# Score matmuls stacked to full contraction height, and vector work reordered, in a fused encoder layer

## The chip, the cores and the metric

One core of a Trainium2 chip runs one program, launched once. The metric is the device time of a run in microseconds (us); each kernel has several runs and their median is given. A profile is one more execution with every instruction recorded.

## What is computed

One encoder layer on x (1 x 1024 x 2048, float32): an RMSNorm, one input projection whose columns feed three mixers, a gate on each mixer, an output projection added to x, and a last RMSNorm.

```python
h = _rmsnorm(x, norm_g[l])
proj = jnp.einsum('bsd,de->bse', h, w_in[l])
ua, va, ga, q, k, v, gb, xc, gc = jnp.split(proj, pts, axis=-1)
ya = _spatial_gating(ua, va, ...)            # 4 groups x 128 channels
yb = _swa_sink_attention(q, k, v, b_sinks[l], rel_bias)
yc = _multiscale_pool(xc, c_w_pool[l], c_scale[l])
mix = jnp.concatenate([ya * silu(ga), yb * silu(gb), yc * silu(gc)], axis=-1)
x = x + jnp.einsum('bse,ed->bsd', mix, w_out[l])
return _rmsnorm(x, final_g)
```

The attention has 16 query heads on 4 key/value heads, 64 channels each. A query chunk of 64 positions sees its own chunk and the one before it, with a relative bias and a sink logit per head:

```python
logits = jnp.einsum('bcqkgd,bcjkd->bckgqj', qb, kb) * 64 ** -0.5 + bias
m = jnp.maximum(jnp.max(logits, -1, keepdims=True), sink)
p = jnp.exp(logits - m)
p = p / (jnp.sum(p, -1, keepdims=True) + jnp.exp(sink - m))
out = jnp.einsum('bckgqj,bcjkd->bcqkgd', p, vb)
```

## The kernel before

**Precision.** TensorE (PE) multiplies fp32r operands. Each float32 operand is split in two: ScalarE (ACT) rounds it to a high part (`split_hi`, L812; `x_hi`, L830) and VectorE (DVE) subtracts to get the low part (`split_lo`, L1106; `x_lo`, L1111). Each product is then three matmuls (`three`, L1561 to L1563): high by high, high by low, low by high.

**Order of the work.** A sequence of 104 groups J of weights (2048 columns of 128 rows) is written out by hand. All engines loop over J, and each executes what its own loop lists, in that order. While PE works on group J, ACT and DVE split group J + 1. Groups 0 to 23 are the first half of the sequence positions (512), 24 to 47 the second half. In a half, g = J mod 24: g = 0 to 3 make k and v, g = 4 to 19 make a tile of q (even g) or of its gate (odd g), g = 20 to 23 a part of mixer A. Groups 48 to 103 are the rest of the projections, and the output projection, done over both halves at once by Strassen-Winograd's seven products: four pairs p = 0 to 3 of 14 steps each, so J = 48 + 14 p + j. Two steps make a product, in the order A12, A11, S2, S1, S4, S3, A22. Each step goes through the four PSUM banks `N[st]`, st = 0 to 3, with 12 matmuls a bank; the odd step ends the product of a bank.

**Banks.** Before the even step of the next product PE waits, bank by bank, until DVE has added the bank into its result (`bank_free` waits on `y_added`). DVE does that in `add_chain`: banks 0 to 2 in the odd step in which PE ends them, bank 3 at the start of the next step. In group 103 the order is different (`last_product`): PE does banks 0 and 1 of groups 102 and 103, then banks 2 and 3 of both, and DVE adds a bank at a time, each followed by ACT's square, the root, and the scaled output rows (`finish_second`).

**Jobs.** The sums of operand blocks that the products need are made along the way by `job`, at groups fixed in the tables `X_AT`, `M_AT` and `S_AT`. A job of kind "s" (r = 0 to 7) makes four sums and splits three tiles, and one of kind "t" splits the other two, one group later (for r = 6 and 7 in the same group). A job of kind "m" splits one tile. The parts go from the buffer `stage` to DRAM by DMAs that the SP queue issues in the next group, and the next job may write `stage` when these have landed (`wait_stored`). SP also loads four operand blocks for each step (`load_s`, 2 MB), the weights, and the tiles `residual` of x, which `add_residual` adds on DVE in steps 8, 11 and 13 of pairs 2 and 3.

**Attention.** At g = 4 the two k tiles (128 rows, two kv heads each) are split (`k_tile_hi`, `k_tile_lo`), and each q tile of two heads at the odd g behind it (`q_tile_hi`, `q_tile_lo`). At the end of the groups g = 5 to 20 PE does `scores` of a piece (two blocks of 128 queries of two heads, 32 pieces in all): for each block three products of 64 rows, for the two heads side by side in the upper and lower rows of the array, 12 matmuls. One group later come its four transposes (`transpose`), two later 16 matmuls with v (`values`). Within a group the order on PE is: projection, values, transposes, scores. DVE brings the scores to `logits` in four instructions (L1292), then maximum and normalisation around ACT's exponentials.

**Start and end.** The sum of squares of x is made by ACT's squares (`x_square`) and GpSimd's (POOL's) sums (L742); ACT may be at most two squares ahead of POOL; the last six squares are in ACT's loop at J = 1, and `split_hi(3)` is among them. `finish_first`, at group 102, scales the finished first half of the rows: a root on ACT, a reciprocal on DVE, then eight scalings on ACT and eight on DVE.

Of the kernel before, what the change touches and what calls it, by code (L numbers as in the profile page):

```python
# [14 lines left out]
P = 128  # L15
# [66 lines left out]
S_AT = (36, 40, 44, 48, step(PAIR_A, 5), step(PAIR_A, 8), step(PAIR_O, 1), step(PAIR_O, 2))  # L82
# [102 lines left out]
def build(nc, x, x_t, w, w_b, norm_g, ln_g, ln_b, w_s, b_s, sinks, rel_bias, one_hot, inv_count, w_pool,  # L185
# [8 lines left out]
    with ExitStack() as ctx:  # L194
# [41 lines left out]
        k_hi = place("k_hi", [P, 2, CHUNK + HS], F32R)  # L236
        k_lo = place("k_lo", [P, 2, CHUNK + HS], F32R)
        at[0] = at_attn + 2 * 4 * KV_HEADS * (CHUNK + HS)
# [485 lines left out]
        def _(pool):  # L724
# [14 lines left out]
            for half in range(HALVES):  # L739
                for kt in range(1, KT):  # L740
                    pool.wait_ge(x_sq_done, KT * half + kt + 1)
                    pool.tensor_tensor(acc[half], acc[half], x_sq[:, kt % 2, :], ALU.add  # L742
                                       ).then_inc(x_acc_done, 1)
                    pool.wait_ge(x_acc_done, (KT - 1) * half + kt)
                if half == 0:
                    pool.wait_ge(consts_loaded, 16 * 10)
                for n in range(PIECES):
                    m = PIECES * half + n
                    if m >= 1:
                        pool.wait_ge(exp_done, 4 * m)  # L750
                    pool.tensor_copy(logits[:, :, P:P + 1].rearrange("p (h t) s -> p h (t s)", t=2),
                                     sink_sb[:, 2 * (n // 2):2 * (n // 2) + 2].unsqueeze(2).broadcast_to([P, 2, 2])
                                     ).then_inc(sink_set, 1)
# [3 lines left out]
        def _(sc):  # L757
# [95 lines left out]
            def k_tile_hi(half, pair):  # L853

                if half == 1:

                    sc.wait_ge(k_saved, 2)
                sc.wait_ge(t_evac, T_TILES * half + pair + 1)
                sc.activation(k_hi[:, pair, CHUNK:CHUNK + HS], k_stage[pair][:, 0:HS], ACT.Copy).then_inc(k_hi_done, 1)

            def q_tile_hi(half, i):
# [6 lines left out]
                sc.activation(q_stack[:, 0, :], q_t[:, 0:HS], ACT.Copy).then_inc(q_hi_done, 1)  # L868
# [112 lines left out]
            for J in range(TOTAL):  # L981
# [12 lines left out]
                if 4 <= J + 1 < TOTAL:  # L994
# [87 lines left out]
                if J == step(PAIR_O + 1, 12):  # L1082
# [9 lines left out]
        def _(ve):  # L1092
# [128 lines left out]
            def add_residual(p, k):  # L1221
# [60 lines left out]
            def softmax_scores(half, n):  # L1282
# [6 lines left out]
                for c in range(2):  # L1289
                    rows = slice(64 * c, 64 * c + 64)  # L1290
                    for a in range(2):
                        last = ve.scalar_tensor_tensor(  # L1292
                            out=logits[rows, 2 * a:2 * a + 2, 0:P],
                            in0=S_bank[a][rows, :].rearrange("p (t s) -> p t s", t=2)[:, :, 64 * c:64 * c + P],
                            scalar=DH ** -0.5, in1=bias[rows, 2 * i + a, :].unsqueeze(1).broadcast_to([64, 2, P]),
                            op0=ALU.mult, op1=ALU.add)
                last.then_inc(scaled, 1)
                ve.wait_ge(scaled, m + 1)
                if half == 0 and tp == 0:

                    settle(ve.memset(logits[0:64, 0:4:2, 0:64], -1e30))
# [4 lines left out]
            def k_tile_lo(half, pair):  # L1306
                ve.wait_ge(k_hi_done, 2 * half + pair + 1)
                ve.tensor_tensor(k_lo[:, pair, CHUNK:CHUNK + HS], k_stage[pair][:, 0:HS],
                                 k_hi[:, pair, CHUNK:CHUNK + HS].bitcast(F32), ALU.subtract).then_inc(k_lo_done, 1)

            def q_tile_lo(half, i):

                ve.wait_ge(q_hi_done, 8 * half + i + 1)
                ve.tensor_tensor(q_stack[:, 1, :], q_t[:, 0:HS], q_stack[:, 0, :].bitcast(F32), ALU.subtract
                                 ).then_inc(q_lo_done, 1)
# [89 lines left out]
            for J in range(TOTAL):  # L1405
# [41 lines left out]
                if half < HALVES and is_t(g - 1):  # L1447
                    ve.wait_ge(group_done, J)
                    if g - 1 == G_Q:

                        ve.wait_ge(k_lo_done, 2 * (half + 1))
# [83 lines left out]
                if p >= 0 and j % 2 == 1 and J < TOTAL - 1:  # L1535
                    add_chain(*divmod((J - IN_GROUPS) // 2, PRODUCTS), range(ST - 1))
# [9 lines left out]
                if J == step(PAIR_O + 1, 12):  # L1546
# [8 lines left out]
        def _(pe):  # L1555
# [184 lines left out]
            def scores(half, n):  # L1740
                i, tp, m = n // 2, n % 2, PIECES * half + n
                pe.wait_ge(q_lo_done, 8 * half + i + 1)
                if n == 0:
                    pe.wait_ge(k_lo_done, 2 * (half + 1))
# [6 lines left out]
                for tl in range(2):  # L1751
                    q0 = P * (2 * tp + tl)
                    for k, (q_part, k_part) in enumerate(((0, k_hi), (0, k_lo), (1, k_hi))):
                        for a in range(2):
# [14 lines left out]
            def values(half, n):  # L1769
# [6 lines left out]
                for tl in range(2):  # L1776
                    st = 2 * tp + tl
                    for a in range(2):
                        kv = 2 * (i // 4) + a
                        d, at = slice(64 * kv, 64 * kv + 64), (2 * a + tl) * P  # L1780
# [130 lines left out]
```

## Time and profile before

| | us |
|---|---|
| median of 3 runs | 1253.82 (1252.9 to 1254.21) |
| the profiled execution: its own time | 1252.9 |
| its span in the trace | 1251.1 |
| PE busy | 1230.0 (98% of the span) |
| PE weight loads busy | 1014.3 (81%) |
| DVE busy | 831.2 (66%) |
| ACT busy | 498.8 (40%) |
| POOL busy | 54.9 (4%) |
| the 16 DMA engines | 69.2% of the span, 251 GB/s |

The profiled execution's own time is 1.8 us above its span. PE's clock was granted in full nearly throughout (0.997 in the mean). Matmuls overlap in the records, so that the distance between two starts, not the length of one, says what a matmul costs.

### The profile page before, as it was taken

To read this page: it belongs to the slowest core of one execution; us is meant where nothing else is said; L and a number is where in the kernel's file an instruction comes from. 1 tells how busy PE (TensorE), PEld (TensorE's weight loads), DVE (VectorE), ACT (ScalarE), POOL (GpSimd) and SP (SyncE) were. 2 spreads that over 40 slices of the span, in tenths; PEclk is the share of its full clock that TensorE was granted. 3 is DMA by queue.
4 is the path that set the end of the run, shared out by engine and by line. 5 is a ranking of instruction groups with operands and counts; after the bars stand their busy time and mean duration, and the time that the engine had idled before them with its cause. 6 is when DMAs were issued, how large, how long until landed. Compare 5 with 4: busy or idle time off the path is not lost.

```text
span 1251.1 us, 16376 instructions
## 1 busy us (share of the span) xinstructions
PE 1230.0 (98%) x6310; PEld 1014.3 (81%) x6310; DVE 831.2 (66%) x1115; ACT 498.8 (40%) x887; POOL 54.9 (4%) x70
## 2 busy tenths in 40 slices
PE   7999999999999999999999999999999999999996
PEld 6878888888988888888888887888888888888884
DVE  7657666664576577776376568777678755665556
ACT  7435454435553354454334112333333512323135
POOL 3400000003110000000000000000000000000000
PEclk9999999999999999999999999999999999999998
DMA  8499446353655256565896877659999799855769
GB/s 312 128 311 332 146 163 210 141 184 124 220 189 211 102 182 222 185 216 201 335 343 225 322 299 270 214 189 356 415 350 354 296 351 395 305 202 204 284 223 332
DMA packets 98813, 314.16 MB, mean 251 GB/s; under 512 B 10128, under 2 KB 13232, under 8 KB 87344
## 3 DMA queue, kind: packets, MB, share of 16 engines
q1 hardware_dynamic: 98736, 313.12, 69.2%
q8 instruction: 50, 0.82, 0.3%
q14 instruction: 27, 0.22, 0.1%
HBM read 241.77 MB, written 71.30 MB: 250 GB/s over the span
## 4 chain that ended last, share of the span: by engine, by line
PE 95%; DMA 2%; DVE 1%; ACT 1%; issue 1%; SPq 0%; ACTq 0%; DVEq 0%
PE n_bank L1561 17%; PE n_bank L1563 17%; PE n_bank L1562 17%; PE t_bank L1561 11%; PE t_bank L1562 10%; PE t_bank L1563 10%; PE e_bank L1561 2%; PE n_bank L1756 2%; PE e_bank L1563 2%; PE e_bank L1562 2%; PE n_bank L1782 2%; PE n_bank L1766 1%; DMA raw<-w_dram 1%; PE e_bank L1796 1%; PE e_bank L1806 1%
## 5 line engine op out<-in xcount | busy, mean ns | idle before, releaser
L1106 DVE TENSOR_TENSOR w_lo<-raw,w_hi 128x1024 fp32r<-128x1024 f32 (+1 forms) x116 | 138.0, 1228 | 153.2 <-ACT w_hi L812 152.9
L1561 PE MATMUL t_bank<-op_hi,w_hi 128*128 128x512 f32 x512 | 203.1, 397 | 0.0
L1562 PE MATMUL t_bank<-op_lo,w_hi 128*128 128x512 f32 x512 | 199.7, 390 | 0.0
L1563 PE MATMUL t_bank<-op_hi,w_lo 128*128 128x512 f32 x512 | 199.4, 389 | 0.0
L812 ACT ACTIVATE w_hi<-raw 128x1024 fp32r<-128x1024 f32 (+1 forms) x116 | 113.2, 1021 | 167.1 <-PE t_bank L1563 111.5
L1561 PE MATMUL n_bank<-s_ring,w_hi 128*128 128x512 f32 x448 | 178.0, 397 | 0.0
L1563 PE MATMUL n_bank<-s_ring,w_lo 128*128 128x512 f32 x448 | 174.4, 389 | 0.0
L1562 PE MATMUL n_bank<-s_ring,w_hi 128*128 128x512 f32 x448 | 174.3, 389 | 0.0
L1561 PE MATMUL n_bank<-w_hi,s_ring 128*128 128x512 f32 x448 | 174.3, 389 | 0.0
L1562 PE MATMUL n_bank<-w_lo,s_ring 128*128 128x512 f32 x448 | 174.3, 389 | 0.0
L1563 PE MATMUL n_bank<-w_hi,s_ring 128*128 128x512 f32 x448 | 174.3, 389 | 0.0
L1561 PEld LDWEIGHTS t_bank<-op_hi,w_hi 128*128 128x128 f32 x512 | 96.3, 188 | 20.5
L1563 PEld LDWEIGHTS t_bank<-op_hi,w_lo 128*128 128x128 f32 x512 | 96.1, 188 | 20.7
L1562 PEld LDWEIGHTS t_bank<-op_lo,w_hi 128*128 128x128 f32 x512 | 96.5, 188 | 17.9
L1562 PEld LDWEIGHTS n_bank<-s_ring,w_hi 128*128 128x128 f32 x448 | 84.1, 188 | 19.1 <-issue 1.9
L1561 PEld LDWEIGHTS n_bank<-s_ring,w_hi 128*128 128x128 f32 x448 | 84.1, 188 | 19.0 <-issue 1.9
L1563 PEld LDWEIGHTS n_bank<-s_ring,w_lo 128*128 128x128 f32 x448 | 84.1, 188 | 17.6
L1562 PEld LDWEIGHTS n_bank<-w_lo,s_ring 128*128 128x128 f32 x448 | 84.1, 188 | 17.6
L1561 PEld LDWEIGHTS n_bank<-w_hi,s_ring 128*128 128x128 f32 x448 | 84.1, 188 | 17.6
L1563 PEld LDWEIGHTS n_bank<-w_hi,s_ring 128*128 128x128 f32 x448 | 84.1, 188 | 17.3
L812 ACT ACTIVATE w_hi<-x_w 128x1024 fp32r<-128x1024 f32 x48 | 48.2, 1051 | 115.0 <-PE n_bank L1563 112.7
L1106 DVE TENSOR_TENSOR w_lo<-x_w,w_hi 128x1024 fp32r<-128x1024 f32 x48 | 56.6, 1219 | 46.3 <-ACT w_hi L812 46.0
(225 smaller groups left out, 1825.7 us busy)
## 6 DMA issues: line engine op xcount, KB each, us to landing
s_ring<-x_parts SPq DMA_DIRECT2D x112, 512.0 KB, 6.1
s_ring<-m_parts SPq DMA_DIRECT2D x112, 512.0 KB, 6.0
raw<-w_dram SPq DMA_DIRECT2D x46, 1024.0 KB, 5.1
y_w<-w_b_dram SPq DMA_DIRECT2D x16, 1024.0 KB, 11.2
mix<-x_t_dram SPq DMA_DIRECT2D x56, 256.0 KB, 5.0
m_parts<-stage SPq DMA_DIRECT2D x24, 512.0 KB, 7.6
x_parts<-stage SPq DMA_DIRECT2D x32, 256.0 KB, 3.0
x_parts<-mix SPq DMA_DIRECT2D x32, 256.0 KB, 3.0
```

Of the source, the lines that this page charges most:

```text
L812: sc.activation(w_hi[:, J % 2, part], w_source(J)[:, part], ACT.Copy).then_inc(hi_done, 1)
L1106: ve.tensor_tensor(w_lo[:, J % 2, part], w_source(J)[:, part], w_hi[:, J % 2, part].bitcast(F32), ALU.subtract).then_inc(lo_done, 1)
L1561: pe.matmul(psum_out, stat[0], mov[0], start=first, stop=False)
L1562: pe.matmul(psum_out, stat[0], mov[1], start=False, stop=False)
L1563: return pe.matmul(psum_out, stat[1], mov[0], start=False, stop=last)
L1756: mm = pe.matmul(S_bank[a][:, 256 * tl:256 * tl + WINDOW], q_stack[rows, q_part, q0:q0 + P], k_part[rows, i // 4, q0:q0 + WINDOW], start=k ...
L1766: mm = pe.transpose(PT_bank[:, P * b:P * b + P], logits[:, b, 0:P], ident[:])
L1782: mm = pe.matmul(O_bank[64 * a:64 * a + 64, P * tl + 64 * c:P * tl + 64 * c + 64], vals[:, st, d], probs_t[:, at + 64 * c:at + 64 * c + 64 ...
L1796: mm = pe.matmul(E[0][:, P * st:P * st + P], mix[:, M_A + j, P * st:P * st + P], w_s_sb[:, j, :], start=True, stop=True)
L1806: pe.matmul(E[1][:], w_pool_sb[:, j, :], aux[:, HIST:HIST + HS], start=True, stop=True).then_inc(pool_ready, 1)
```

## The change

Seven edits, in one diff. The scores take operands of 128 rows: `q_stack` holds for each head the high part of q in its own 64 rows and the low part in the other 64, and `k_hi` and `k_lo` hold each kv head's part in both halves of the rows, so that two matmuls a head and block give all four products of the parts; 8 matmuls a piece. The splits of k and q write 64 rows at a time. The scores are brought to `logits` in two instructions. The wait and place of `split_hi(3)` change. `add_chain` of banks 0 to 2 stands behind the jobs and the residuals in DVE's loop. One job "s" (and its "t") moves a group later. `finish_first` moves from group 102 to 101.

```diff
-S_AT = (36, 40, 44, 48, step(PAIR_A, 5), step(PAIR_A, 8), step(PAIR_O, 1), step(PAIR_O, 2))
+S_AT = (36, 40, 44, 48, step(PAIR_A, 6), step(PAIR_A, 8), step(PAIR_O, 1), step(PAIR_O, 2))
...
-        k_hi = place("k_hi", [P, 2, CHUNK + HS], F32R)
-        k_lo = place("k_lo", [P, 2, CHUNK + HS], F32R)
+        k_hi = place("k_hi", [P, KV_HEADS, CHUNK + HS], F32R)
+        k_lo = place("k_lo", [P, KV_HEADS, CHUNK + HS], F32R)
...
-                sc.activation(k_hi[:, pair, CHUNK:CHUNK + HS], k_stage[pair][:, 0:HS], ACT.Copy).then_inc(k_hi_done, 1)
+                for a in range(2):
+                    for to in (a, 1 - a):
+                        sc.activation(k_hi[64 * to:64 * to + 64, 2 * pair + a, CHUNK:CHUNK + HS],
+                                      k_stage[pair][64 * a:64 * a + 64, 0:HS], ACT.Copy).then_inc(k_hi_done, 1)
...
-                sc.activation(q_stack[:, 0, :], q_t[:, 0:HS], ACT.Copy).then_inc(q_hi_done, 1)
+                for a in range(2):
+                    rows = slice(64 * a, 64 * a + 64)
+                    sc.activation(q_stack[rows, a, :], q_t[rows, 0:HS], ACT.Copy).then_inc(q_hi_done, 1)
...
-                if 4 <= J + 1 < TOTAL:
+                if 3 <= J + 1 < TOTAL:
                     split_hi(J + 1)
...
                     for kt in range(KT - SQUARES_LAG, KT):
                         x_square(0, kt)
-                        if kt == KT - 4:
-                            split_hi(3)
...
-                if J == step(PAIR_O + 1, 12):
+                if J == step(PAIR_O + 1, 11):
                     finish_first()
...
                 elif k == 1:
-                    ve.wait_ge(y22_added, 8 * p + 2 * ST - 1)
-                elif p < PAIRS - 1:
-                    ve.wait_ge(y_added, added(p, Q_A22, ST - 2))
+                    ve.wait_ge(y22_added, 8 * p + ST)
                 else:
                     ve.wait_ge(y_added, added(p, Q_S3, ST - 1))
...
+                    last = ve.scalar_tensor_tensor(
+                        out=logits[rows, :, 0:P],
+                        in0=n_banks[rows, 0:2, :].rearrange("p t (a s) -> p (t a) s", a=2)[:, :, 64 * c:64 * c + P],
...
             def k_tile_lo(half, pair):
...
+                for a in range(2):
+                    own = slice(64 * a, 64 * a + 64)
+                    ve.wait_ge(k_hi_done, 8 * half + 4 * pair + 2 * a + 1)
+                    for to in (a, 1 - a):
+                        ve.tensor_tensor(k_lo[64 * to:64 * to + 64, 2 * pair + a, CHUNK:CHUNK + HS],
+                                         k_stage[pair][own, 0:HS],
+                                         k_hi[own, 2 * pair + a, CHUNK:CHUNK + HS].bitcast(F32),
+                                         ALU.subtract).then_inc(k_lo_done, 1)
...
+                for a in range(2):
+                    ve.wait_ge(q_hi_done, 16 * half + 2 * i + a + 1)
+                    own, other = slice(64 * a, 64 * a + 64), slice(64 - 64 * a, 128 - 64 * a)
+                    ve.tensor_tensor(q_stack[other, a, :], q_t[own, 0:HS], q_stack[own, a, :].bitcast(F32),
+                                     ALU.subtract).then_inc(q_lo_done, 1)
...
-                if p >= 0 and j % 2 == 1 and J < TOTAL - 1:
-                    add_chain(*divmod((J - IN_GROUPS) // 2, PRODUCTS), range(ST - 1))
                 for t, kind, i in JOBS:
                     if t == J:
                         job(kind, i)
                 for k, t in enumerate((8, 11, 13)):
                     if p >= PAIR_O and j == t:
                         add_residual(p, k)
+                if p >= 0 and j % 2 == 1 and J < TOTAL - 1:
+                    add_chain(*divmod((J - IN_GROUPS) // 2, PRODUCTS), range(ST - 1))
...
-                for tl in range(2):
-                    q0 = P * (2 * tp + tl)
-                    for k, (q_part, k_part) in enumerate(((0, k_hi), (0, k_lo), (1, k_hi))):
-                        for a in range(2):
-                            rows = slice(64 * a, 64 * a + 64)
-                            mm = pe.matmul(S_bank[a][:, 256 * tl:256 * tl + WINDOW], q_stack[rows, q_part, q0:q0 + P],
-                                           k_part[rows, i // 4, q0:q0 + WINDOW], start=k == 0, stop=k == 2)
+                for a in range(2):
+                    for tl in range(2):
+                        q0 = P * (2 * tp + tl)
+                        for part in (k_hi, k_lo):
+                            mm = pe.matmul(S_bank[tl][:, 256 * a:256 * a + WINDOW], q_stack[:, a, q0:q0 + P],
+                                           part[:, 2 * (i // 4) + a, q0:q0 + WINDOW], start=part is k_hi,
+                                           stop=part is k_lo)
```

The layout of `logits` changes from head by block to block by head with it (the sink's copy on POOL, the masked quarter, and `values` follow), and the counts of the semaphores follow the new numbers of instructions. `finish_first` moves in both ACT's and DVE's loop.

## Rows read from the trace of the kernel before

**Rows 1.** The page's fourth part: the chain that ended last, by engine.

```profile
PE 95%; DMA 2%; DVE 1%; ACT 1%; issue 1%; SPq 0%; ACTq 0%; DVEq 0%
```

**Rows 2.** Busy time by stretch: the last 34 us.

```profile
1217.00:1251.10 34.10, 21.85 (x97) 17.76 (x95) 21.80 (x37) 20.80 (x40) 0.00 (x0) 0.89 0.91 333
```

**Rows 3.** Timeline of PE: start, length, line, operation; one attention piece (n=2).

```profile
118.09 0.66 PE L1766 MATMUL n_bank<-ident,probs 128*128 128x128 f32 x4
118.68 0.36 PE L1756 MATMUL n_bank<-k_hi,q_stack 64*128 64x192 f32 x2
118.87 0.28 PE L1756 MATMUL n_bank<-k_lo,q_stack 64*128 64x192 f32 x2
...
119.32 0.28 PE L1756 MATMUL n_bank<-k_hi,q_stack 64*128 64x192 f32 x2
119.53 0.50 PE L1561 MATMUL t_bank<-op_hi,w_hi 128*128 128x512 f32 x1
119.86 0.39 PE L1562 MATMUL t_bank<-op_lo,w_hi 128*128 128x512 f32 x1
```

**Rows 4.** Timeline of PE: transposes with no scores behind them.

```profile
289.90 0.66 PE L1766 MATMUL n_bank<-ident,probs 128*128 128x128 f32 x4
...
290.63 0.39 PE L1562 MATMUL e_bank<-w_lo,op_hi 128*128 128x512 f32 x1
```

**Rows 5.** Timeline of PE: matmuls of 256 columns and 128 rows.

```profile
13.01 0.28 PE L1561 MATMUL n_bank<-w_hi,op_hi 128*128 128x256 f32 x1
13.13 0.28 PE L1562 MATMUL n_bank<-w_lo,op_hi 128*128 128x256 f32 x1
```

**Rows 6.** Last square on ACT; POOL's 15 sums; PE's first matmul of group 3.

```profile
43.54 0.64 ACT L851 ACTIVATE x_sq<-mix 128x512 f32<-128x512 f32 x1 [1.30 <-POOL rstd_row L742]
...
L742 POOL TENSOR_TENSOR rstd_row<-rstd_row,x_sq x15: 1297/1627/2295, 19.4 to 44.9; 128x512 f32<-128x512 f32 x15
...
43.67 0.28 PE L1561 MATMUL n_bank<-w_hi,op_hi 128*128 128x256 f32 x1
```

**Rows 7.** Low part of q on DVE and the scores behind it, group 29.

```profile
377.93 0.69 DVE L1314 TENSOR_TENSOR q_stack<-q_t,q_stack 128x512 fp32r<-128x512 f32 x1 [0.77 <-ACT q_stack L868]
...
381.80 0.36 PE L1756 MATMUL n_bank<-k_hi,q_stack 64*128 64x192 f32 x2
```

**Rows 8.** PE's first matmuls of groups 70 and 102, 32 groups apart.

```profile
868.76 0.39 PE L1561 MATMUL n_bank<-s_ring,w_hi 128*128 128x512 f32 x1
...
1216.93 0.39 PE L1561 MATMUL n_bank<-w_hi,s_ring 128*128 128x512 f32 x1
```

**Rows 9.** Issue to landing: the store issued at 858.4, the residual at 1217.9.

```profile
DMA to landing us min/median/max: 8.3/8.3/8.3
...
DMA to landing us min/median/max: 8.6/8.6/8.6
```

**Rows 10.** Timeline of DVE in groups 71, 75, 77, 89 and 103.

```profile
891.02 1.29 DVE L1127 TENSOR_TENSOR c<-c,stage 128x512 f32<-128x512 f32 x2 [2.34 <-ACT stage L881]
...
936.39 0.69 DVE L1127 TENSOR_TENSOR stage<-t,stage 128x512 fp32r<-128x512 f32 x1 [0.28 <-ACT stage L881]
...
953.88 0.68 DVE L1127 TENSOR_TENSOR stage<-t,stage 128x512 fp32r<-128x512 f32 x1
...
960.41 0.68 DVE L1185 TENSOR_TENSOR t<-n_bank,t 128x512 f32<-128x512 f32 x1
...
1085.83 2.29 DVE L1235 TENSOR_TENSOR t<-t,residual 128x2048 f32<-128x2048 f32 x1 [1.28 <-DMA residual<-x_dram]
...
1228.35 2.29 DVE L1235 TENSOR_TENSOR y<-y,residual 128x2048 f32<-128x2048 f32 x1
...
1232.89 0.68 DVE L1185 TENSOR_TENSOR y<-n_bank,y 128x512 f32<-128x512 f32 x1
```

**Rows 11.** Timeline of ACT: the table load and the scaling in group 102.

```profile
1222.27 1.28 ACT L783 ACT_TABLE_LOAD   x1
...
1224.11 2.56 ACT L790 ACTIVATE t<-t,rstd_y 128x512 f32<-128x512 f32 x4 [0.25 <-DVE rstd_y L1365]
```

More of the change, by code:

```diff
@@ L750, in _ @@
                         pool.wait_ge(exp_done, 4 * m)
-                    pool.tensor_copy(logits[:, :, P:P + 1].rearrange("p (h t) s -> p h (t s)", t=2),
-                                     sink_sb[:, 2 * (n // 2):2 * (n // 2) + 2].unsqueeze(2).broadcast_to([P, 2, 2])
+                    pool.tensor_copy(logits[:, :, P:P + 1].rearrange("p (t h) s -> p t (h s)", t=2),
+                                     sink_sb[:, 2 * (n // 2):2 * (n // 2) + 2].unsqueeze(1).broadcast_to([P, 2, 2])
                                      ).then_inc(sink_set, 1)
@@ L1290, in softmax_scores @@
                     rows = slice(64 * c, 64 * c + 64)
-                    for a in range(2):
[L1292 to L1296, printed above, removed]
+                    last = ve.scalar_tensor_tensor(
+                        out=logits[rows, :, 0:P],
+                        in0=n_banks[rows, 0:2, :].rearrange("p t (a s) -> p (t a) s", a=2)[:, :, 64 * c:64 * c + P],
+                        scalar=DH ** -0.5,
+                        in1=bias[rows, 2 * i:2 * i + 2, :].rearrange("p a s -> p (a s)").unsqueeze(1).broadcast_to([64, 2, 2 * P]),
+                        op0=ALU.mult, op1=ALU.add)
                 last.then_inc(scaled, 1)
@@ L1299, in softmax_scores @@
                 if half == 0 and tp == 0:
-                    settle(ve.memset(logits[0:64, 0:4:2, 0:64], -1e30))
+                    settle(ve.memset(logits[0:64, 0:2, 0:64], -1e30))
                 ve.wait_ge(sink_set, m + 1)
@@ L1306, in k_tile_lo @@
             def k_tile_lo(half, pair):
-                ve.wait_ge(k_hi_done, 2 * half + pair + 1)
-                ve.tensor_tensor(k_lo[:, pair, CHUNK:CHUNK + HS], k_stage[pair][:, 0:HS],
-                                 k_hi[:, pair, CHUNK:CHUNK + HS].bitcast(F32), ALU.subtract).then_inc(k_lo_done, 1)
-            def q_tile_lo(half, i):
-                ve.wait_ge(q_hi_done, 8 * half + i + 1)
-                ve.tensor_tensor(q_stack[:, 1, :], q_t[:, 0:HS], q_stack[:, 0, :].bitcast(F32), ALU.subtract
-                                 ).then_inc(q_lo_done, 1)
+                for a in range(2):
[6 more added lines that the diff above has]
+                                         ALU.subtract).then_inc(k_lo_done, 1)
+            def q_tile_lo(half, i):
+                for a in range(2):
[3 more added lines that the diff above has]
+                                     ALU.subtract).then_inc(q_lo_done, 1)
             def softmax_norm(half, n):
@@ L1449, in _ @@
                     if g - 1 == G_Q:
-                        ve.wait_ge(k_lo_done, 2 * (half + 1))
+                        ve.wait_ge(k_lo_done, 8 * (half + 1))
                     take(half, g - 1, q_t[:, 0:HS] if (g - 1 - G_Q) % 2 == 0 else pre[:, 0:HS])
@@ L1545, in _ @@
                         weigh(i)
-                if J == step(PAIR_O + 1, 12):
+                if J == step(PAIR_O + 1, 11):
                     finish_first()
@@ L1741, in scores @@
                 i, tp, m = n // 2, n % 2, PIECES * half + n
-                pe.wait_ge(q_lo_done, 8 * half + i + 1)
+                pe.wait_ge(q_lo_done, 16 * half + 2 * i + 2)
                 if n == 0:
-                    pe.wait_ge(k_lo_done, 2 * (half + 1))
+                    pe.wait_ge(k_lo_done, 8 * (half + 1))
                     pe.wait_ge(v_evac, ST * (half + 1))
@@ L1748, in scores @@
                     pe.wait_ge(scaled, m)
-                for tl in range(2):
-                    q0 = P * (2 * tp + tl)
-                    for k, (q_part, k_part) in enumerate(((0, k_hi), (0, k_lo), (1, k_hi))):
-                        for a in range(2):
-                            rows = slice(64 * a, 64 * a + 64)
-                            mm = pe.matmul(S_bank[a][:, 256 * tl:256 * tl + WINDOW], q_stack[rows, q_part, q0:q0 + P],
-                                           k_part[rows, i // 4, q0:q0 + WINDOW], start=k == 0, stop=k == 2)
+                for a in range(2):
[5 more added lines that the diff above has]
+                                           stop=part is k_lo)
                 mm.then_inc(s_ready, 1)
@@ L1779, in values @@
                         kv = 2 * (i // 4) + a
-                        d, at = slice(64 * kv, 64 * kv + 64), (2 * a + tl) * P
+                        d, at = slice(64 * kv, 64 * kv + 64), (2 * tl + a) * P
                         for c, vals in enumerate((v_prev, v)):
```

1 line of the change is left out of this document (removed).

## The prediction

> **What bounds the kernel.** I read the page's chain first: 95% of what ended last is PE [rows 1]. The stretches come next. From 8.4 to 1217 us PE has no long gap, so until then only what shortens PE's stream or makes it wait counts; in the last 34 us PE is busy for 21.9, and the end belongs to DVE and ACT [rows 2]. Then the timeline of PE around one attention piece, to price the scores [rows 3 to 5]. Last, what each PE group waits for, and how late DVE comes to it: the change alters DVE's order in the odd steps, and PE's bank wait stands behind each of them. Group starts are 10.88 apart: from 868.76 (group 70) to 1216.93 (group 102) are 32 of them [rows 8]. So group 72 starts at 890.52, 76 at 934.04, 78 at 955.80, 90 at 1086.37.
>
> **Scores on PE.** From the start of the transposes at 118.09 to the second projection matmul behind the scores at 119.86 pass 1.77 us [rows 3]. Where no scores stand between, the same way takes 290.63 - 289.90 = 0.73 [rows 4]. So a piece costs 1.04, though its six side-by-side pairs are only 0.11 apart (118.87 to 119.32 is four of them) [rows 3]. The other 0.37 sits around the borders: the first pair comes 0.19 before the second, and the first projection matmul takes 0.33 to the second instead of 0.23. I read it as the price of going from 128 rows to 64 and back. The new piece has 8 matmuls of 128 rows and 192 columns. No such one is in the trace; the four transposes (128 columns) pass at 0.10 each [rows 4], 256 columns at 0.12 [rows 5]. I take 0.11, since 192 lies between: 0.88, a gain of 0.16 in each of 32 pieces, 5.0 us. The ends: 8 x 0.10 gives 7.7, 8 x 0.12 gives 2.6.
>
> The Trainium skill speaks against this edit: TensorE: Matmul & The Clock Gate, Part 3 (Packing small matmuls), says that matmuls of few rows in different row groups run concurrently, at nearly the price of one. By that alone full rows lose, 8 slots for 6. TensorEngine Tiling (Array Packing), Key Properties, has the other side, "Mode switching requires drain". The trace shows both, pairs that start together and 0.37 at the borders; which weighs more is a matter of the rows above, and the first page alone is a rival below.
>
> **Splits of k and q.** Instructions of 64 rows are taken as long as those of 128 (0.69 on DVE, 0.60 from start to start, as the two in 1.29 show [rows 10]). At g = 4 DVE has eight instead of two, ACT eight instead of two; DVE is done 6 x 0.60 = 3.6 later. In group 4 the slack covers it. In group 28 DVE has a layer norm behind it and no idle time until q: today the low part of q ends at 378.6, and the scores start at 381.80 [rows 7]. It starts 3.6 later, waits about 0.77 for ACT as now, and has a second instruction: 378.6 + 3.6 + 0.6 = 382.8. PE would come at 381.7, half a border sooner than now: a stall of 1.1 (0 to 1.5). In the other q groups over 5 us of slack hide 0.6 on each engine. Two instead of four instructions for the scores lie beside PE: nothing.
>
> **split_hi(3).** PE needs group 3 at 43.67 [rows 6]. The last square starts at 43.54, held by POOL; POOL's sums took up to 2.30 when DVE worked beside them and 1.30 at best [rows 6]. The split now comes behind it. Without the split between, the last three sums are some 2 us faster together: last square 41.5, high part from 42.1 to 43.1, the low part's first half (1.2 to 2.1 on DVE) by 45.0. Stall 1.4; if POOL gains nothing, 44.1 + 1.1 + 2.1 = 47.3 and 3.6; at best 0.6.
>
> **Adds behind jobs and residuals.** `add_chain` frees bank 0 for PE at the next even step. Where DVE waits for a transfer first, PE now waits too.
> - *Group 70* (job t4, now in group 69). The stage must be free: the store of s4 is issued at 858.4, and one issued then landed 8.3 later [rows 9]: 866.7. ACT and DVE need 0.66 and 1.29 more, the two adds 1.28: 869.9. By the offset in group 71 (first split 891.02, 11.4 after its group's start) it is 871.8. PE wants 868.76: stall 1.1 to 3.1, taken 2.2.
> - *Group 72* (t5). The splits end at 892.3 [rows 10], an add is 0.68: 892.9 against 890.52, 2.4. The stores of t4 now come a group later and hold s5 by about 0.5 more; taken 2.6 (0.8 to 3.2).
> - *Group 76* (m14, m15). Their low parts end at 937.0 [rows 10], the add at 937.7 against 934.04: 3.7 (3.3 to 4).
> - *Group 78* (s6, t6). The jobs run from 953.88 to 960.41, 6.5 [rows 10]. They now start about 6.0 after group 77's start; 6.0 + 6.5 + 0.7 = 13.2 against 10.88: 2.3 (1.5 to 3). This one is no transfer, but DVE's own length.
> - *Group 90.* The residual lands at 1085.8, its add takes 2.29, then 0.68: 1088.8 against 1086.37 [rows 10]: 2.4 (2 to 2.8).
> - Groups 62 and 88 have work before the adds too, but the transfers are in, and PE's need is over 0.9 later: nothing. DVE's later work has over 4 us of slack at every split. Job s4 at the even step 68 lies before nothing that PE needs soon.
>
> **The end.** In group 101 the sums of squares are ready. ACT's table load (1.28) goes ahead of its wait. Its eight scalings take 2 x 2.5 [rows 11] and run until about 1221.4, ahead of `split_hi(103)`, so that split's low part is ready at 1223.7, and PE needs it at 1216.93 + 2 x 2.72 = 1222.37: a stall of 1.4. It costs the end little: PE's last matmul today starts before DVE's last adds, by 4 us. DVE is free for the last residual at 1224.9, which was issued at 1217.9 and lands 8.6 later, 1226.5 [rows 9]; today its add starts at 1228.35, and bank 0 at 1232.89 [rows 10]. So the chain of the last four banks (3.3 each) starts 1.85 earlier; bank 2, delayed on PE, comes to the same point. Gain 1.85 (0.9 to 2).
>
> **Sum.** -5.0 for scores, +1.1 and +1.4 in the first stages, +2.2 + 2.6 + 3.7 + 2.3 + 2.4 = +13.2 at the banks, -1.85 at the end: +8.85. On the profiled execution's own 1252.9 that is 1261.7. It stood 0.9 below the median; the forecast is 1262.
>
> **Rivals.**
> - *Transfers land sooner (the other side).* Every stage store and the residual land in a time that the trace gives for one layout of traffic. PE's delay spreads that traffic, and stores that land 3.7 earlier in a group would let the jobs end before PE asks. Then groups 70, 72, 76 and 90 lose nothing: 10.9 less, 1251, and with group 3's stall gone too 1249. For it: each stall leaves the queues more time. Against: SP issues the stores when PE starts a group, so they move with PE. It decides at a landing under 4.6 from the issue; the trace has 8.3 to 10.
> - *Borders stay.* The 0.37 is not from the rows in use but from scores as such. Then 8 x 0.11 replaces 6 x 0.11, +0.22 x 32 = +7.1 instead of -5.0: 1274. For it: pairs that start 0.11 apart cost no more than one matmul would. Against: the transposes give way to 128-row matmuls with no border at all [rows 4]. This rival is what Part 3 of the Trainium skill's page TensorE: Matmul & The Clock Gate would make of the edit.
> - *DVE passes through the jobs faster*, by a job's wait that was idle time of ACT and is no more: half of the bank stalls. Then 1255.5, hardly to be told from before.
>
> **Chances.** The forecast's case 0.80, own range 1256.5 to 1266.5 (the ends of the terms taken together, not all at once). Sooner transfers 0.09, borders 0.04, faster jobs 0.07. Faster by over 0.2% (2.5 us, about what a measurement can tell) 0.07, within 0.11, slower 0.82. The range 1255 to 1267 leaves out the first two rivals.
>
> **What would show it.** Scores: 8 matmuls 0.11 apart, and 0.23 from the first projection matmul to the second. PE's idle time ahead of the first matmuls of groups 70, 72, 76, 78, 90 with DVE's add as releaser, and of group 3's split. Banks of 0 stall at 76 and 90 would make the prediction wrong at once; so would scores that cost over 1 us. A stall before the scores of group 29 decides the k split, and bank 0's last add before 1232 plus the shift the end.

## The result, and the profile after

| | before | after |
|---|---|---|
| median in the comparison on one chip, us | 1253.53 | 1274.67 (1270.99 to 1276.23) |
| ratio | | 1.0165, 95% interval 1.014 to 1.0188 |
| profiled execution: own time, span | 1252.9, 1251.1 | 1271.56, 1269.7 |

The change costs 21.1 us; 1262 was forecast, with 1255 to 1267 as the range. The direction was right, the size was not: the loss is more than twice the forecast one. A wait of PE is in what follows the distance between the matmuls on either side of it, less the 0.23 at which they otherwise follow each other. Line numbers differ by a few after the change: L1568 to L1570 are the three matmuls, L1187 is DVE's addition of a bank.

The chain that ended last now holds less PE than in [rows 1], 80%:

```profile
PE 80%; DMA 7%; DVE 5%; ACT 3%; issue 2%; POOL 1%; SPq 1%; ACTq 0%; DVEq 0%; POOLq 0%
```

What PE waited for, total, times, longest (waits view of after):

```profile
PE n_bank L1568 <- DVE t L1187: 12.1, 5, 3.9
PE n_bank L1568 <- DVE op_lo L1113: 8.2, 1, 8.2
PE n_bank L1568 <- DVE w_lo L1108: 2.5, 2, 1.3
PE n_bank L1762 <- DVE q_stack L1321: 2.3, 1, 2.3
```

The second line is the start of the kernel. The five waits of the first line stand at groups 70, 72, 76, 78 and 90, as forecast.

The attention piece of [rows 3]. The scores are 0.11 apart, and the projection matmul behind them takes 0.25 to the next, not 0.33:

```profile
119.43 0.66 PE L1773 MATMUL n_bank<-ident,probs 128*128 128x128 f32 x4
119.84 0.34 PE L1762 MATMUL n_bank<-k_hi,q_stack 128*128 128x192 f32 x1
120.02 0.27 PE L1762 MATMUL n_bank<-k_lo,q_stack 128*128 128x192 f32 x1
120.13 0.28 PE L1762 MATMUL n_bank<-k_hi,q_stack 128*128 128x192 f32 x1
...
120.80 0.42 PE L1568 MATMUL t_bank<-op_hi,w_hi 128*128 128x512 f32 x1
121.05 0.39 PE L1569 MATMUL t_bank<-op_lo,w_hi 128*128 128x512 f32 x1
```

From the transposes to that second matmul pass 121.05 - 119.43 = 1.62, against 1.77: 0.15 less in each piece. Only the first score stands further from the next (119.84 to 120.02, 0.18), as before the change (0.19).

Group 29, DVE and then PE. Before, DVE had two instructions for k_lo and one for q_stack [rows 7]:

```profile
369.59 2.84 DVE L1311 TENSOR_TENSOR k_lo<-q_t,k_hi 64x512 fp32r<-64x512 f32 x4
372.46 2.84 DVE L1311 TENSOR_TENSOR k_lo<-x_raw,k_hi 64x512 fp32r<-64x512 f32 x4
...
382.48 1.40 DVE L1321 TENSOR_TENSOR q_stack<-q_t,q_stack 64x512 fp32r<-64x512 f32 x2 [0.77 <-ACT q_stack L872]
```

```profile
381.27 0.39 PE L1570 MATMUL e_bank<-op_hi,w_lo 128*128 128x512 f32 x1
383.94 0.36 PE L1762 MATMUL n_bank<-k_hi,q_stack 128*128 128x192 f32 x1 [2.29 <-DVE q_stack L1321]
...
385.33 0.68 PE L1568 MATMUL t_bank<-op_hi,w_hi 128*128 128x512 f32 x1
385.81 0.63 PE L1569 MATMUL t_bank<-op_lo,w_hi 128*128 128x512 f32 x1
```

Four instructions of 64 rows take 2.84, the last one 0.69 of it, so they start 0.72 apart, where 0.60 was assumed. PE waits 2.67 - 0.23 = 2.4. Then it is slow: the last two matmuls stand 0.48 apart instead of the 0.25 above. The stretches tell why (start and end, length, PE busy, PE loads, DVE, ACT, POOL, granted clock, DMA share, GB/s; first of before, then of after):

```profile
376.00:393.00 17.00, 17.00 (x84) 13.84 (x84) 12.21 (x21) 6.22 (x13) 0.19 (x1) 1.00 0.81 310
```

```profile
376.00:393.00 17.00, 14.71 (x62) 11.94 (x62) 14.62 (x23) 6.93 (x15) 0.10 (x1) 0.90 0.82 314
889.00:907.00 18.00, 14.14 (x57) 11.28 (x56) 13.88 (x14) 8.55 (x9) 0.00 (x0) 0.91 1.03 401
936.00:952.00 16.00, 12.58 (x44) 9.86 (x43) 9.14 (x10) 4.75 (x6) 0.00 (x0) 0.79 0.95 362
```

A granted clock of 0.90 in the mean over 17 us is (1 - 0.90) x 2 x 17 = 3.4 us at the lower level, 1.2 GHz, the rest at 2.4. In the same way there are about 3.2 us of it behind the wait of group 72, and 6.7 behind that of group 76. Before, no stretch up to the last product is at the lower level.

Group 72. Before, DVE began job s5 without a wait:

```profile
874.75 0.69 DVE L1127 TENSOR_TENSOR stage<-c,stage 128x512 fp32r<-128x512 f32 x1
```

After, ACT and DVE:

```profile
884.02 0.63 ACT L885 ACTIVATE stage<-c 128x512 fp32r<-128x512 f32 x1 [11.25 <-DMA m_parts<-c]
```

```profile
884.75 0.69 DVE L1129 TENSOR_TENSOR stage<-c,stage 128x512 fp32r<-128x512 f32 x1 [5.85 <-ACT stage L885]
...
888.87 1.29 DVE L1129 TENSOR_TENSOR c<-c,stage 128x512 f32<-128x512 f32 x2 [0.77 <-ACT stage L885]
890.27 2.36 DVE L1108 TENSOR_TENSOR w_lo<-y_w,w_hi 128x1024 fp32r<-128x1024 f32 x2
892.55 2.28 DVE L1181 TENSOR_TENSOR y_w<-z_w,y_w 128x2048 f32<-128x2048 f32 x1
894.87 1.29 DVE L1129 TENSOR_TENSOR c<-c,stage 128x512 f32<-128x512 f32 x2
896.08 2.47 DVE L1187 TENSOR_TENSOR t<-n_bank,t 128x512 f32<-128x512 f32 x4
```

```profile
m_parts<-stage SPq DMA_DIRECT2D x2, 256.0 KB, 10.7
m_parts<-c SPq DMA_DIRECT2D x2, 256.0 KB, 10.8
```

The last two lines are the DMA view of 868 to 880: t4's stores, issued from 871.05 on, took 10.5 to 11.1 to land. So job s5, which needs the buffer, starts at 884.0 on ACT, and DVE has stood idle for 5.85 before it. With the split, the weight sum and t5 behind it DVE is then busy nearly without a gap until the addition at 896.1, for which PE has been waiting since 892.8.

The whole difference, from the distance between the last matmuls of one group and the next in both profiled executions. The wait ahead of the scores of group 29 falls into the length of group 30:

| place | forecast | measured |
|---|---|---|
| scores, 32 pieces | -5.0 | -4.9 |
| group 3 | +1.4 | +1.56 |
| group 28 | 0 | +0.25 |
| group 30 | +1.1 | +4.2 |
| group 70 | +2.2 | +0.54 |
| group 72 | +2.6 | +5.55 |
| group 76 | +3.7 | +6.35 |
| group 78 | +2.3 | +2.54 |
| group 90 | +2.4 | +2.58 |
| small differences | 0 | +0.6 |
| PE starts group 102 later by | 10.7 | 19.3 |
| the end | -1.85 | -0.7 |
| the span | +8.85 | +18.6 |

The median is some 3 us above the profiled execution; the mean granted clock is 0.991 in it and 0.989 in the slowest one (1276.23).

### The profile page after: what moved, and what is told of

Same layout as the page of the kernel before. It is cut to its first block, busy times and chain, and to the rows that moved or that the text cites. A ratio compares the mean times of both kernels' runs of the same rounds, so it can differ in the third digit from the quotient of the medians.

```text
span 1269.7 us, 16115 instructions
## 1 busy us (share of the span) xinstructions
PE 1234.1 (97%) x6182; PEld 1022.3 (81%) x6182; DVE 843.7 (66%) x1079; ACT 519.1 (41%) x915; POOL 52.6 (4%) x70
## 4 chain that ended last, share of the span: by engine, by line
PE 80%; DMA 7%; DVE 5%; ACT 3%; issue 2%; POOL 1%; SPq 1%; ACTq 0%; DVEq 0%; POOLq 0%
PE n_bank L1568 14%; PE n_bank L1570 14%; PE n_bank L1569 14%; PE t_bank L1568 9%; PE t_bank L1569 9%; PE t_bank L1570 9%; PE n_bank L1762 2%; DMA raw<-w_dram 2%; PE n_bank L1789 2%; DMA residual<-x_dram 2%; PE n_bank L1773 1%; DMA mix<-x_t_dram 1%; DVE w_lo L1108 1%; PE e_bank L1568 1%; PE e_bank L1569 1%
## 5 line engine op out<-in xcount | busy, mean ns | idle before, releaser
L1568 PE MATMUL t_bank<-op_hi,w_hi 128*128 128x512 f32 x512 | 201.5, 393 | 0.0
L1570 PE MATMUL t_bank<-op_hi,w_lo 128*128 128x512 f32 x512 | 200.2, 391 | 0.0
L1568 PE MATMUL n_bank<-w_hi,s_ring 128*128 128x512 f32 x448 | 175.9, 393 | 9.2 <-DVE t L1187 8.0
L1568 PE MATMUL n_bank<-s_ring,w_hi 128*128 128x512 f32 x448 | 178.9, 399 | 4.1 <-DVE t L1187 4.1
L1570 PE MATMUL n_bank<-w_hi,s_ring 128*128 128x512 f32 x448 | 175.3, 391 | 0.0
L1570 PE MATMUL n_bank<-s_ring,w_lo 128*128 128x512 f32 x448 | 174.9, 390 | 0.0
L1570 PEld LDWEIGHTS t_bank<-op_hi,w_lo 128*128 128x128 f32 x512 | 96.6, 189 | 20.5
L1568 PEld LDWEIGHTS t_bank<-op_hi,w_hi 128*128 128x128 f32 x512 | 97.1, 190 | 18.3
L1568 PEld LDWEIGHTS n_bank<-w_hi,s_ring 128*128 128x128 f32 x448 | 84.7, 189 | 28.5 <-DVE t L1187 9.2
L1568 PEld LDWEIGHTS n_bank<-s_ring,w_hi 128*128 128x128 f32 x448 | 84.5, 189 | 24.0 <-DVE t L1187 5.0
L1569 PEld LDWEIGHTS n_bank<-w_lo,s_ring 128*128 128x128 f32 x448 | 84.8, 189 | 17.6
L1570 PEld LDWEIGHTS n_bank<-w_hi,s_ring 128*128 128x128 f32 x448 | 84.7, 189 | 17.6
L1570 PEld LDWEIGHTS n_bank<-s_ring,w_lo 128*128 128x128 f32 x448 | 84.4, 188 | 17.8
```

Of the source, the lines that this page charges most:

```text
L1568: pe.matmul(psum_out, stat[0], mov[0], start=first, stop=False)
L1569: pe.matmul(psum_out, stat[0], mov[1], start=False, stop=False)
L1570: return pe.matmul(psum_out, stat[1], mov[0], start=False, stop=last)
```

## Experiments

Each is compared with the kernel before on the same chip. The changed kernel was not run again beside them, so "less than the changed kernel" is against its 1274.67; the kernel before took 1253.53 to 1253.79 in all comparisons. "Group n" with a time is the distance from the last matmul of group n - 1 to that of group n; 10.88 is the undisturbed value of groups 67 to 101.

**1. Additions first again.** The changed kernel with

```diff
+                if p >= 0 and j % 2 == 1 and J < TOTAL - 1:
+                    add_chain(...)
                 for t, kind, i in JOBS:
...
-                if p >= 0 and j % 2 == 1 and J < TOTAL - 1:
-                    add_chain(...)
```

and `S_AT` and the waits of `add_residual` as before.

> The changed kernel with DVE's additions of banks 0 to 2 put back ahead of the jobs and residuals (and job s4 back in group 67). Theory A (PE waits for the additions, and the granted clock falls behind two of the waits): groups 70, 72, 76, 78 and 90 each come back to 10.88, which takes off 0.54 + 5.55 + 6.35 + 2.54 + 2.58 = 17.6 us: 1274.7 - 17.6 = 1257.1, and the granted clock is 2.4 GHz in 860 to 1200. Theory B (the prediction's account, in which the order of the additions costs 13.2 and the rest of the miss lies elsewhere): 1261.5. The stall in group 29 stays in both: about 2.5 us ahead of the scores and 3.4 us at 1.2 GHz behind it.

1256.57, ratio 1.0021 (1.0012 to 1.003): 18.1 less than the changed kernel. Groups 70, 72, 76, 78 and 90 are 10.88. Theory A holds, 13.2 was too little. Three things came otherwise: group 102 takes 21.7, not 17.8 (experiment 4); group 3 takes 17.6, with the lower clock behind its wait of 2.3; and no lower clock follows the wait of 2.2 in group 29.

**2. No idle PE in the waits.** In `pair_step`, ahead of `bank_free`:

```diff
+FILL = {72: 17, 76: 15, 78: 10, 90: 10}
+                    if st == 0 and J in FILL:
+                        split_ready(J, 0)
+                        for _ in range(FILL[J]):
+                            pe.matmul(T[0][:], w_tile(w_hi, J % 2, 0, P), w_tile(w_hi, J % 2, 0, 512),
+                                      start=True, stop=True)
```

> The changed kernel, but PE passes idle matmuls (128x512 of the group's weights into a bank that nothing reads) just ahead of its wait for bank 0: 17 in group 72, 15 in group 76, 10 each in groups 78 and 90, at 0.23 each a little less than the stalls. Nothing of the result changes. Theory A (the clock falls because PE stood idle): DVE's additions come when they came before, so the groups' first matmuls start as late as in the changed kernel, but no stretch at 1.2 GHz follows; groups 72 and 76 take 1.5 and 2.8 less: 4.3 off, 1274.7 to 1270.4 in the median and less spread between executions (if slower executions are those in which the clock also fell at 78 or 90, the gain is up to 6). Theory B (the clock falls there for another reason, or the 1.5 and 2.8 are late operands and not the clock): no gain, 1274 to 1275, and the same lengths of groups 72 and 76.

1266.9 (1266.15 to 1269.35), ratio 1.0107 (1.0093 to 1.0121): 7.8 less than the changed kernel, by adding 52 useless matmuls. The same two stretches:

```profile
889.00:907.00 18.00, 18.00 (x81) 14.69 (x79) 15.72 (x17) 8.54 (x10) 0.00 (x0) 1.00 1.03 397
936.00:956.00 20.00, 19.12 (x85) 15.50 (x84) 10.58 (x12) 6.36 (x6) 0.00 (x0) 1.00 0.97 342
```

The clock stays at 2.4 GHz. Group 72 takes 14.9 instead of 16.4. Group 76 takes 15.5 instead of 17.2, though its additions came 1.0 later than in the changed kernel. Theory A holds: what was lost beyond the waits is the clock, and it fell because PE stood idle. The Trainium skill, TensorE: Matmul & The Clock Gate, Part 1, says that the clock of the array follows how busy it has lately been; the trace agrees. The gain in the median exceeds the 4.3 of the two falls in the profile and the 6 that was expected at most: part of it may be falls elsewhere (behind the wait of group 29, for one, the clock stayed at 2.4 GHz in this profile), which filled waits do not explain. The two profiled executions are only 2.2 apart, because group 3 took 19.6 here against 15.2: its wait was 3.2, and the clock fell.

**3. Job s4 back alone.** `S_AT` with `step(PAIR_A, 5)`, everything else as changed.

> The changed kernel with job s4 alone back in group 67 (t4 in 68). Theory A (the excess in group 72 comes from the stores of t4, which hold s5 back, and s5, the split, the weight sum and t5 follow one another on DVE): t4's stores are issued a group sooner, s5 is no longer held, the stall in group 72 goes from 4.0 to the 2.4 of the prediction, the 0.5 at group 70 goes, and the total falls by 2 (or by 3.5, if the clock then doesn't fall in group 72): 1271 to 1272.7. Theory B (t5 is late for a reason of its own, DVE's weight sum and split ahead of it): group 72 stays at 16.4 us, and the total falls by 0.5 at most.

1265.94, ratio 1.0097 (1.0082 to 1.0112): 8.7 less, where 2 to 3.5 was expected. Group 72 takes 11.8 instead of 16.4, group 70 is back at 10.88, and group 68 pays 1.4 for s4. Theory A has the cause, for DVE no longer stands idle before s5, but not the size: the wait in group 72 falls to 0.8, not to 2.4. The stores that t5 waits for landed at 891.3 and PE asked for its bank at 893.2, later by group 68's wait; in the kernel before the two times were 890.4 and 890.5. Between the two profiled executions, 6.8 apart, these three groups make 3.8 and group 76 makes 1.4 (0.4 less wait, and 3.4 us at 1.2 GHz instead of 6.8); the rest of the 8.7 in the medians is not accounted for by a wait that the edit touches.

**4. A version of its own.** Stacked scores, `finish_first` in 101, additions first, `split_hi(3)` as before, and the second k tile later:

```diff
                     k_tile_lo(half, 0)
-                    k_tile_lo(half, 1)
...
                     q_tile_lo(half, (g - 1 - G_Q) // 2)
+                    if g - 1 == G_Q:
+                        k_tile_lo(half, 1)
...
                 if n == 0:
-                    pe.wait_ge(k_lo_done, 8 * (half + 1))
+                    pe.wait_ge(k_lo_done, 8 * half + 4)
...
+                if n == PIECES // 2:
+                    pe.wait_ge(k_lo_done, 8 * (half + 1))
```

> The stacked scores and finish_first in group 101, with the additions ahead of the jobs, split_hi(3) among the squares as before, and the low parts of the second k tile moved on DVE from group 28 to group 29, behind the low part of q; PE waits for them at piece 8 only. Theory A (the stall ahead of the first scores is DVE's four more instructions of 64 rows for the second k tile, 2.84 us): no stall in group 29, nor a fall of the clock; scores -4.9, end -2.1, group 3 as before: 1253.5 - 7.0 = 1246.5. Theory B (the stall belongs to the 64-row splits as such, of q and of the first tile, or to ACT): 1.5 to 4 of it stay, 1248 to 1250.5.

1249.99, ratio 0.9973 (0.9964 to 0.9981). That is in theory B's range, but not for its reason. The wait in group 29 is gone, as by theory A; one of 0.6 comes in its place at the end of group 30, where DVE is later by these instructions. But group 102 takes 21.7:

```profile
1218.21 0.39 PE L1580 MATMUL n_bank<-w_hi,s_ring 128*128 128x512 f32 x1
1222.11 0.47 PE L1578 MATMUL n_bank<-w_hi,s_ring 128*128 128x512 f32 x1 [3.52 <-DVE w_lo L1110]
```

DVE's additions in group 101 wait for PE bank by bank, 2.7 apart, before `finish_first` may start; so the scalings end later and `split_hi(103)` with them: PE has a wait of 3.7 in group 102, and the lower clock behind it. In the changed kernel, with the additions behind the residual, they ran through in 3.7 in all. That was a benefit of the new order, in this one group.

**5. The scores alone, and the order of group 101.** The first is experiment 4 with `finish_first` in 102 again. The second is experiment 4 with one exception (and that residual's wait as in the changed kernel):

```diff
-                if p >= 0 and j % 2 == 1 and J < TOTAL - 1:
+                adds = p >= 0 and j % 2 == 1 and J < TOTAL - 1
+                if adds and J != step(PAIR_O + 1, 11):
                     add_chain(...)
...
                         add_residual(p, k)
+                if J == step(PAIR_O + 1, 11):
+                    add_chain(...)
```

> The kernel before with the stacked scores alone, the second k tile's low parts in group 29: no other edit of the change. Theory A (32 pieces at 0.153 less each, 4.9, and a wait of 0.6 ahead of the transposes in group 30, since DVE is later by the four instructions): 1253.6 - 4.9 + 0.6 = 1249.3, with the end as before (bank 0's last addition 5 us sooner). Theory B (the end is held by the residual's transfer and not by PE, so that the 4.9 is partly given back there): 1250.5 or more.

> As the kernel with finish_first in group 101 and the additions first, but in group 101 alone DVE does the residual first and then the additions, as in the changed kernel. Theory A (finish_first started late there because DVE's three additions wait for PE bank by bank; behind the residual they run through in 3.7 us): the wait in group 102 shrinks from 5.4 to 1.4, no fall of the clock, and the last banks come about 2 us sooner: 1247.3. Theory B (the wait in group 102 is the eight scalings of finish_first as such): group 102 stays at 21.7 and the time at 1250.

The scores alone: 1249.4, ratio 0.9963 (0.995 to 0.9977). With the order of group 101: **1247.01, ratio 0.9946 (0.9934 to 0.9959)**, 6.8 faster than the kernel before and, by the ratios 0.9946 and 1.0165, 2.2% faster than the changed one. Both as theory A had them. Group 102 is 17.76 again, and DVE waits 1.8 for the last residual, not 3.5 as in the changed kernel:

```profile
1216.45 1.28 DVE L1189 TENSOR_TENSOR y<-n_bank,y 128x512 f32<-128x512 f32 x2
1218.21 2.36 DVE L1110 TENSOR_TENSOR w_lo<-x_w,w_hi 128x1024 fp32r<-128x1024 f32 x2 [0.48 <-ACT w_hi L811]
1222.34 2.29 DVE L1239 TENSOR_TENSOR y<-y,residual 128x2048 f32<-128x2048 f32 x1 [1.77 <-DMA residual<-x_dram]
```

So moving `finish_first`, with this order in group 101, is worth 2.4 (1249.4 - 1247.0).

**6. `split_hi(3)` alone,** in the kernel before.

> The kernel before with split_hi(3) behind the squares, nothing else. Theory A (a wait of PE of 1.4 ahead of group 3, behind which the granted clock falls in some executions, as group 3 took 15.2, 14.7, 17.6 and 19.6 in four profiles of kernels with this edit): 1253.6 + 1.1 to 1.5 where the clock holds and up to 6 where it falls, median 1255.5 to 1257, spread wider than before. Theory B (the prediction's account: the wait alone): 1255.0, spread as before.

1256.54 (1255.31 to 1258.57), ratio 1.0022 (1.0013 to 1.0031): +2.75 where the wait alone makes 1.35 (group 3: 15.0 in the profile). The three executions at 1255.3 have a mean granted clock of 0.996 to 0.997, the four from 1256.6 to 1257.2 have 0.995 or 0.997 and the slowest 0.996, so the clock may explain the excess only in part. Theory B, with the spread as before (1252.64 to 1254.46), falls; A is not fully shown. The two profiles in which the clock fell behind this wait took 17.6 and 19.6 in group 3 (experiments 1 and 2), but their waits were 2.3 and 3.2. Over five profiles of kernels with this edit the last square started between 41.3 and 43.1 and the wait was 0.9 to 3.2, so a longer wait is a second reason for slow executions, and nothing here tells the two apart.

**7. The order alone.** The kernel before with the additions behind jobs and residuals and s4 in group 68.

> The kernel before with DVE's additions behind jobs and residuals, and job s4 in group 68: no other edit. Theory A (these two edits alone make the waits of groups 70, 72, 76, 78, 90, and the falls of the granted clock behind the longest): the five groups take 17.6 more together, 1253.7 + 17.6 = 1271.3, or 1.5 to 3 less or more with the number of falls. Theory B (the prediction's account, 13.2): 1266.9. Theory C (the waits need the other edits beside them): under 1264.

1270.37, ratio 1.0132 (1.0115 to 1.0149): +16.7, near theory A's 17.6. The waits need nothing of the other edits. In the profile the five groups make 15.8 of it, and group 72's wait of 3.6 passed without the lower clock, group 76's of 3.2 did not (6.8 us of it).

**8. What a wait costs PE.** Idle additions on DVE in the kernel before, three sets of doses:

```diff
+DOSE = {83: 10, 91: 8, 95: 10, 97: 9, 99: 12}
+                if J in DOSE:
+                    for k in range(DOSE[J]):
+                        settle(ve.tensor_tensor(T[0][:], final_g_sb[:, 0:512], final_g_sb[:, 512:1024], ALU.add))
                 if p >= 0 and j % 2 == 1 and J < TOTAL - 1:
                     add_chain(...)
```

> The kernel before with idle additions on DVE (128x512, into a bank that nothing reads) ahead of the additions of banks 0 to 2: 10 in group 83, 8 in 91, 10 in 95, 9 in 97, 12 in 99. PE's waits at bank 0 of the next even groups come to about 3.0 (84), 1.4 (92), 2.8 (96), 2.3 (98) and 4.2 (100). Theory A (the length of the wait decides whether the granted clock falls): group 100 loses a further 1.5 or more at 1.2 GHz, 84 and 96 perhaps, 92 and 98 nothing beyond the wait. Theory B (it falls at certain places or times, whatever the wait): no order by length.

> As the kernel with idle additions on DVE, the numbers swapped over the places: 13 in group 83, 12 in 91, 9 in 95, 13 in 97, 9 in 99. By the 0.73 an addition measured there, PE waits 3.7 in group 84, 4.6 in 92, 2.4 in 96, 3.7 in 98 and 2.5 in 100. Theory A (length decides): the clock falls behind 84, 92 and 98, and not behind 96, perhaps behind 100. Theory B (place decides): again behind group 100 alone.

> Once more: 12 idle additions in group 83, 10 in 91, 12 in 95, 12 in 97, 11 in 99; PE's waits about 3.0 in group 84, 3.1 in 92, 4.6 in 96, 2.9 in 98 and 3.9 in 100. Theory A (length decides): the clock falls behind 96 and 100; the three of about 3 lie where both outcomes were seen (3.15 without, 3.19 with). Theory B (place decides): behind group 100 alone.

They took 1267.79, 1277.8 and 1280.68 in one execution each. The wait of PE, and the group's length beyond 10.88 and the wait, where the clock fell:

| group | first set | second | third |
|---|---|---|---|
| 84 | 1.49 | 3.69 | 2.96, fell, +3.0 |
| 92 | 1.68 | 4.61, fell, +2.7 | 3.15 |
| 96 | 3.15 | 2.42, fell, +1.8 | 4.61, fell, +2.3 |
| 98 | 0.76 | 3.70, fell, +1.8 | 2.96, fell, +1.8 |
| 100 | 4.69, fell, +1.7 | 2.49 | 3.96, fell, +1.7 |

Two stretches of the third set, groups 84 and 92, with waits of 2.96 and 3.15:

```profile
1020.00:1034.00 14.00, 11.20 (x37) 8.69 (x36) 13.76 (x18) 2.00 (x2) 0.00 (x0) 0.76 0.88 360
1112.00:1124.00 12.00, 9.01 (x40) 7.16 (x39) 11.72 (x15) 2.00 (x2) 0.00 (x0) 1.00 0.49 175
```

Theory B (place) falls: each of the five places is seen with a fall and without. Theory A holds at the ends only: no wait under 2 us was followed by a fall, all of 3.9 and more were (5 with the changed kernel's). In between it failed: in the second set the clock held behind 3.69 and fell behind 2.42. Between 2.2 and 3.7 it fell behind 13 of 26 waits, counted over the profiles of all these kernels. What decides there is open.

What a fall costs is clearer. The slow stretches were 3.4 or 6.8 long, and some began while PE still waited; the cost is half of the part in which PE has work. In the third set the 6.8 of group 84 lay with 6.2 behind the wait: half is 3.1, measured 3.0. The 6.8 of group 96 began 2.1 before the wait ended: half of the 4.7 left is 2.35, measured 2.3.

## Why the prediction was right in direction and wrong in size

The failed step: every stall was entered as PE's waiting time alone (+1.1, +1.4, and +13.2 at the banks). What was left out is that the granted clock falls to 1.2 GHz behind some of them. In the profiled execution that is 1.6 in group 30, 1.5 in group 72 and 2.8 in group 76: 5.9 of the 9.8 by which the span's growth (18.6) exceeds the forecast 8.85, and, by the lower mean clock of the slower executions, probably part of the further 3 us of the median; that part is not shown. The rest of the 9.8 is the waits of groups 29 and 72 (1.3 and 1.4 more than forecast, against 1.7 less at group 70), 1.2 less gained at the end, and some 1.7 in small differences. The sum's last step had a slip too: 1252.9 + 8.85 and the 0.9 to the median make 1262.7, not 1262.

Two agreements are luck. The measured 1274.67 is the 1274 of the rival of staying borders, whose mechanism the trace excludes. And the waits at the banks add up to 13.0 against 13.2 only because the forecast was 1.7 too high for group 70 and 1.4 too low for group 72.

- **Scores** (-5.0): right, 0.153 in each of 32 pieces, 4.9. The border is gone behind the scores and the 0.11 for 192 columns was right. The rival of staying borders is out; the trace has both of its parts, pairs 0.11 apart before and full rows 0.11 apart after, and here the border weighs more. Where it sat was read in part wrongly: the 0.19 from the first score to the second stays (0.18), and the gain lies ahead of the first score and behind the last.
- **Splits of k and q** (+1.1): the place and the cause right, the wait 2.4. The spacing was mis-sized: six more at 0.72 and a second one for q at 0.72 make 5.0, not 4.2; DVE started 0.2 later in group 28, and PE came 0.2 sooner. The lower clock added 1.6. Moving half of the k split one group on removes it (experiment 4).
- **`split_hi(3)`** (+1.4): 1.56 in the profile, the last square at 41.67 against the 41.5 assumed. Alone it costs 2.75 in the median, more than its wait.
- **Group 70** (+2.2): 0.5. The 2.2 was the middle of two estimates, 1.1 and 3.1. The lower one had the mechanism, and the store that t4 waited for, issued at 860.17, landed after 7.5 instead of 8.3.
- **Group 72** (+2.6): the wait is 4.0. "Hold s5 by about 0.5 more" was wrong. I had followed t4's stores to their landing but not what queued on DVE behind the late s5: split, weight sum and t5 each ahead of the additions. DVE stood idle for 5.85 before s5, and the stores took up to 11.1. In experiment 3, without the s4 edit, that idle time is gone and PE waits 0.8.
- **Groups 76, 78, 90** (+3.7, +2.3, +2.4): waits of 3.6, 2.4 and 2.45, each within 0.1. The rival of sooner transfers is out: it needed landings under 4.6, and they were 7.5 in group 70 and over 10 in group 72; the residual held DVE for 6.5 in group 89, and no job ended before PE asked.
- **The end** (-1.85): 0.7 in the changed kernel. PE's wait of 1.4 in group 102 is hidden as forecast; but the last residual, issued at 1237.6, reached DVE only at 1247.54, 9.9 later instead of 8.6. In experiment 5 it took 8.8 (1213.56 to 1222.34), and moving `finish_first` is worth 2.4.

```profile
1237.60 0.43 SPq L614 DMA_DIRECT2D residual<-x_dram  x1
```

```profile
1247.54 2.29 DVE L1235 TENSOR_TENSOR y<-y,residual 128x2048 f32<-128x2048 f32 x1 [3.53 <-DMA residual<-x_dram]
```

The third rival, a faster DVE, needed half of the bank stalls to vanish; 13.0 of the 13.2 stood there.

Open: what decides whether the clock falls behind a wait of 2.2 to 3.7 us, why the slower executions of the `split_hi(3)` kernel are slow, and how each execution's falls add to the median. No more than one execution of a kernel has a profile.

## What to carry to other kernels

An engine's order list is a priority list: work that frees another engine's buffer stands ahead of work that waits for a transfer, and the exception (group 101) is where the freeing work itself waits and something else can pass it. Where a bound engine gets a new wait of over 2 us, price it as the wait plus 1.5 to 3 us of slow clock with a chance of about a half, and count on it from 4 us on, as all five waits of 3.96 to 4.69 here had it; a kernel at 98% PE has nothing to absorb it. When a step is moved later, follow what it delays through the in-order queue of each engine to the next buffer release, not only to its own end.

## What the runs showed of the hardware beyond that

- PE doing useless matmuls while it waits made the kernel 7.8 us faster: the granted clock stayed at 2.4 GHz through 4.0 us of waiting in group 72.
- Behind a wait, 3.4 us at 1.2 GHz cost 1.5 to 1.8 and 6.8 us cost 2.3 to 3.0. Equal waits (4.61 twice, 2.96 twice) were not followed by equal losses.
- DVE's splits of 64 rows stand 0.72 apart, each starting 0.03 behind the end of the one before. The additions of 128 rows and the same 512 columns stand 0.60 apart, the two splits of k before the change 0.66: they overlap. The length of one is 0.69 either way, so halving the rows saved nothing and doubled the number. Rows alone are not the reason: some instructions of 128 rows (L1279) stand 0.72 apart too.
- t4's stores landed 10.5 to 11.1 after their issue, the four issued from 858.43 on before the change 8.3 to 9.6 [rows 9]. The DMA engines were busy throughout in both stretches, so that alone does not make the difference. After the change two weight loads were under way when the stores were issued (they landed at 873.6 and 876.0), before it one (861.5); that this held the stores up is not shown.
